# A two-block transformer layer on one core: expert weights in six ring places and six side places, side places used in every pair of experts

## What is computed

```python
def hierarchical_moe(h, w_rg, b_rg, w_re, b_re, w1, w3, w2):
    # per token: the best of 4 groups, in it the best 2 of 8 experts, weights e_w
    ...
    def expert_block(args):
        xb, e = args
        hid = jax.nn.silu(xb @ w1[e]) * (xb @ w3[e])     # 1024 -> 512
        return hid @ w2[e]                               # 512 -> 1024
    ...

def first_block(x, ...):
    ...                                                  # attention and a gated convolution
    h2 = modulate(rms_norm(x, g_norm2[l]), sh2, sc2)
    x = x + ga2[:, None, :] * hierarchical_moe(h2, ...)
    return x

def reference(...):
    x = first_block(...)
    return second_block(x, ...)                          # recurrent mixer, attention, FFN, PLE
```

## Time and profile before

| | before |
|---|---|
| median of 3 runs | 1196.93 us (1193.87 to 1198.81) |
| the profiled execution's span | 1196.8 us, its own time within 0.1 us of the median |
| PE busy | 1148.5 us (96%) |
| DVE, ACT, POOL busy | 481.1, 410.5, 222.0 us |
| moved by DMA | 331.68 MB, mean 277 GB/s |
| chain that ended last | PE 73%, DMA 16%, DVE 6%, issue 2%, ACT 2% |
| largest DMA part of the chain | ring<-in_w (expert weights), 15% |

### The profile page before, as it was taken

The page is one execution under the profiler, slowest core; times in us unless marked ns, Lnnn a source line. Parts: engine busy times, 40 slices in busy tenths (PEclk is TensorE's granted clock), DMA queues, the critical chain, the costliest instruction groups (busy, mean ns, idle before and its releaser), DMA issues.

```text
span 1196.8 us, 15588 instructions
## 1 busy us (share of the span) xinstructions
PE 1148.5 (96%) x5930; PEld 761.6 (64%) x5930; DVE 481.1 (40%) x971; ACT 410.5 (34%) x609; POOL 222.0 (19%) x100
## 2 busy tenths in 40 slices
PE   4999999999999999999989998999999999999998
PEld 2678867774444444444434435978877788888886
DVE  3475552753222222222212215589454653323226
ACT  3533454232111111111111115664245363444334
POOL 0163333300000000000000002200313444443522
PEclk8899999999999999999999998999999999999999
DMA  9897366689899999999999996453223464645541
GB/s 355 322 329 264 128 229 246 269 329 367 339 377 421 423 422 421 422 422 422 422 420 421 422 421 240 160 192 126 86 71 141 150 194 159 210 147 181 201 163 48
DMA packets 92329, 331.68 MB, mean 277 GB/s; under 512 B 3937, under 2 KB 26754, under 8 KB 66674
## 3 DMA queue, kind: packets, MB, share of 16 engines
q1 hardware_dynamic: 91648, 330.36, 71.2%
q0 software_dynamic: 432, 0.48, 0.2%
q10 hardware_dynamic: 194, 0.06, 0.0%
HBM read 329.84 MB, written 1.05 MB: 276 GB/s over the span
## 4 chain that ended last, share of the span: by engine, by line
PE 73%; DMA 16%; DVE 6%; issue 2%; ACT 2%; SPq 0%; DVEq 0%; ACTq 0%
DMA ring<-in_w 15%; PE ps L839 14%; PE ps L840 13%; PE ps L841 13%; PE ps L1196 13%; PE ps L1238 5%; PE ps L1168 1%; PE ps L1169 1%; DVE ring_r L1992 1%; PE ps L912 1%; DMA ring<-in_w_ada 1%; ACT ring_r L1550 1%; PE ps L1349 1%; PE ps L976 1%; PE ps L974 1%
## 5 line engine op out<-in xcount | busy, mean ns | idle before, releaser
L814 POOL TENSOR_TENSOR ring_r<-ring,ring_r 128x1024 fp32r<-128x1024 f32 x76 | 197.8, 2623 | 824.5 <-ACT ring_r L1550 824.4
L1196 PE MATMUL ps<-ring,arena 128*64 128x512 f32 x1008 | 226.0, 596 | 8.8 <-DMA ring<-in_w 7.7
L840 PE MATMUL ps<-ring_r,hl_r 128*128 128x512 f32 x528 | 211.4, 400 | 0.0
L839 PE MATMUL ps<-ring_r,hl_r 128*128 128x512 f32 x480 | 197.5, 411 | 10.7 <-DVE hr_r L2085 6.1
L841 PE MATMUL ps<-ring_r,hr_r 128*128 128x512 f32 x480 | 192.0, 400 | 0.0
L1550 ACT ACTIVATE ring_r<-ring 128x2048 fp32r<-128x2048 f32 x90 | 167.4, 1907 | 62.5 <-PE ps L841 45.0
L1196 PEld LDWEIGHTS ps<-ring,arena 128*64 128x64 f32 x1008 | 69.5, 137 | 149.0 <-issue 127.6
L1992 DVE TENSOR_TENSOR ring_r<-ring,ring_r 128x2048 fp32r<-128x2048 f32 x52 | 121.3, 2339 | 84.5 <-ACT ring_r L1550 84.3
L839 PEld LDWEIGHTS ps<-ring_r,hl_r 128*128 128x128 f32 x480 | 91.8, 191 | 41.2 <-issue 14.7
L840 PEld LDWEIGHTS ps<-ring_r,hl_r 128*128 128x128 f32 x528 | 101.0, 191 | 21.9
L841 PEld LDWEIGHTS ps<-ring_r,hr_r 128*128 128x128 f32 x480 | 91.8, 191 | 22.3
(11 more groups left out here) (370 smaller groups left out, 1650.7 us busy)
## 6 DMA issues: line engine op xcount, KB each, us to landing
ring<-in_w SPq DMA_DIRECT2D x91, 2048.0 KB, 21.5
ring<-in_w_in SPq DMA_DIRECT2D x21, 2048.0 KB, 8.4
ring<-in_w_ada SPq DMA_DIRECT2D x16, 1024.0 KB, 10.2
ring<-in_w_ffn_gate SPq DMA_DIRECT2D x11, 1024.0 KB, 5.2
ring<-in_w_ffn_up SPq DMA_DIRECT2D x11, 1024.0 KB, 7.8
ring<-in_w_ffn_down SPq DMA_DIRECT2D x5, 2048.0 KB, 7.8
ring<-in_w_ada SPq DMA_DIRECT2D x4, 2048.0 KB, 8.7
ring<-in_w_o SPq DMA_DIRECT2D x2, 2048.0 KB, 7.7
```

The costliest lines, as they stand in the source:

```text
L814: nc.gpsimd.tensor_tensor(rest[:, a:b], w[:, a:b], lead[:, a:b].bitcast(F32), ALU.subtract).then_inc(sem("w_rest_b"), 1)
L839: mm(o, lhsT=a_lead, rhs=b_lead, start=start, stop=False, skip_group_check=True)
L840: mm(o, lhsT=a_lead, rhs=b_rest, start=False, stop=False, skip_group_check=True)
L1196: last = mm(H[slots_of(e), :], lhsT=xs[:, k, slots_of(e)], rhs=w, start=k == 0, stop=k == KD - 1)
```

## The change

It touches three engines.

- **Places.** `early_w2` now holds w2 of every even pair, and `early_w1` chunk 0 of every odd pair. In the ring, slots 4, 1 and 2 (chunks 0, 4 and 5) then hold only every other pair's chunk, so there they are free a pair earlier.
- **SP.** The first transfer into `spp` is issued when the router's logits have been read (`small.released["lgt1"]`), ahead of that into `x`, which still waits for the first gather. From pair 3 on, `pair_loads` issues a pair's loads. For pairs 3 to 8 the order is chunks 0, 4, 5, 1, 2, 3, from pair 9 on 0 to 5. Chunks 0, 4 and 5 wait for pair i - 2, chunks 1, 2 and 3 for pair i - 1 as before.
- **PE.** Turns 0 to 11 are one loop of two turns (an even, an odd), run six times; turns 12 to 15 are written out behind the branch.
- **POOL.** The clearing of `scT` waits for `moe_ys1_done` at 15 instead of 3.

```diff
-        BESIDE = {0: (1,), 4: (0, 2), 5: (0, 2)}
+        BESIDE = {0: 1, 4: 0, 5: 0}
...
-            landed[slot] += 16 * (PAIRS - len(BESIDE.get(n, ())))
+            landed[slot] += 16 * (PAIRS // 2 if n in BESIDE else PAIRS)
...
+        def pair_loads(sp_, i, odd, order):
+
+            for n in order:
+                if odd and n == 0:
+                    sp_.wait_ge(*block_used(0, i - 1))
+                    for e in range(2):
+                        early_w1_load(sp_, i, e)
+                elif not odd and n == 4:
+                    sp_.wait_ge(sem("moe_ys1_done"), i - 1)
+                    for e in range(2):
+                        early_w2_load(sp_, i, e)
+                elif odd or n < 4:
+                    sp_.wait_ge(*block_used(n, i - 1 if n in BESIDE else i))
+                    expert_load(sp_, n, i, chunk_in)
...
+            sp_.wait_ge(*small.released["lgt1"])
+            early_w1_load(sp_, 1, 1)
             sp_.wait_ge(sem("moe_gather1_done"), 1)
-            early_w1_load(sp_)
+            early_w1_load(sp_, 1, 0)
...
-            with sp_.Fori(3, PAIRS) as i:
-                for n in range(6):
-                    sp_.wait_ge(*block_used(n, i))
-                    expert_load(sp_, n, i, chunk_in)
+            with sp_.Fori(1, AHEAD_TWOS) as j:
+                for n in (1, 2):
+                    pair_loads(sp_, 2 * j + n, n == 1, (0, 4, 5, 1, 2, 3))
+            with sp_.Fori(AHEAD_TWOS, PAIRS // 2 - 1) as j:
+                for n in (1, 2):
+                    pair_loads(sp_, 2 * j + n, n == 1, range(6))
+            pair_loads(sp_, PAIRS - 1, True, range(6))
...
-            pool.wait_ge(sem("moe_ys1_done"), 3)
+            pool.wait_ge(sem("moe_ys1_done"), PAIRS - 1)
...
                 if early:
-                    pe.wait_ge(sem("early_w2_in"), 64 * early)
+                    pe.wait_ge(sem("early_w2_in"), 64 * half_i + 64)
...
-            turn(0, 0, 0, 1)
-            turn(1, 0, 0)
-            turn(2, 0, 0, 2)
-            with pe.Fori(3, PAIRS - LATE_TURNS) as i:
-                turn(i, 0, 0)
+            with pe.Fori(0, (PAIRS - LATE_TURNS) // 2) as j:
+                turn(2 * j, j, 0, 0, False)
+                turn(2 * j + 1, j, 0, 0, True)
 
             def late_turns():
-                with pe.Fori(PAIRS - LATE_TURNS, PAIRS - 1) as i:
-                    turn(i, 0, 0)
-                last_turn(PAIRS - 1, 0, 0)
+                for i in range(PAIRS - LATE_TURNS, PAIRS - 1):
+                    turn(i, i // 2, 0, 0, i % 2 == 1)
+                last_turn(PAIRS - 1, PAIRS // 2 - 1, 0, 0, True)
```

More of the change, by code:

```diff
@@ L34 @@
 LATE_TURNS = 4
+AHEAD_TWOS = 4
 DFF = 2816
@@ L564, in two_blocks, with in_ring @@
             moe_in_base.append(landed[slot] + 16)
-            landed[slot] += 16 * (PAIRS - len(BESIDE.get(n, ())))
+            landed[slot] += 16 * (PAIRS // 2 if n in BESIDE else PAIRS)
             busy[slot] = sem("moe_" + name), 2 * PAIRS - 1 + n % 2 if n < 4 else PAIRS
-        def in_ring(n, i):
-            beside = BESIDE.get(n, ())
-            return moe_in_base[n] + 16 * (i - (sum(b < i for b in beside) if isinstance(i, int) else len(beside)))
+        def in_ring(n, i, half_i):
+            return moe_in_base[n] + 16 * (half_i if n in BESIDE else i)
         def block_used(n, pairs):
@@ L706, in expert_load, with early_w1_load @@
             sp_.dma_start(view, src).then_inc(signal[MOE_SLOT[n]], 16)
[L708 to L712, removed]
+        def early_w1_load(sp_, pair, e):
+            w = expert_w[0][bass.ds(2 * pair + e, 1)]
+            src = w.rearrange("e (h p j) n -> h p (e j n)", p=P, j=4)
+            sp_.dma_start(early_w1[e], src[0]).then_inc(sem("early_w1_in"), 16)
         def early_w2_load(sp_, pair, e):
-            src = expert_w[4][2 * pair + e].rearrange("(h p j) n -> h p (j n)", p=P, j=2)
+            w = expert_w[4][bass.ds(2 * pair + e, 1)]
+            src = w.rearrange("e (h p j) n -> h p (e j n)", p=P, j=2)
             for h in range(2):
                 sp_.dma_start(early_w2[2 * e + h], src[h]).then_inc(sem("early_w2_in"), 16)
+        def pair_loads(sp_, i, odd, order):
[11 more added lines that the diff above has]
+                    expert_load(sp_, n, i, chunk_in)
         block = ctx.enter_context(nc.Block())
@@ L1173, in slots_of, with chunk_ready @@
                 return slice(e * CAP, (e + 1) * CAP)
-            def chunk_ready(n, i, done):
+            def chunk_ready(n, i, half_i, done):
                 if done:
@@ L1178, in chunk_ready, with up @@
                 else:
-                    pe.wait_ge(chunk_in[MOE_SLOT[n]], in_ring(n, i))
-            def up(n, H, i, done, beside=False):
+                    pe.wait_ge(chunk_in[MOE_SLOT[n]], in_ring(n, i, half_i))
+            def up(n, H, i, half_i, done, odd):
+                beside = odd and n == 0 and not done
                 for h in range(2):
                     if beside and h == 0:
-                        pe.wait_ge(sem("early_w1_in"), 32)
+                        pe.wait_ge(sem("early_w1_in"), 32 * half_i + 32)
                     else:
-                        chunk_ready(2 * n + h, i, done)
+                        chunk_ready(2 * n + h, i, half_i, done)
                     if n == 0:
@@ L1213, in w2_rows, with middle @@
                 return ring[:, MOE_SLOT[4 + f // 2], at:at + COL]
-            def middle(i, done, col0, more_pairs, early=0):
+            def middle(i, half_i, done, col0, more_pairs, odd):
+                early = not odd and not done
                 places(i, done, col0)
-                up(1, HB, i, done)
+                up(1, HB, i, half_i, done, odd)
                 if more_pairs:
@@ L1233, in middle @@
                     if not early:
-                        chunk_ready(4 + h, i, done)
+                        chunk_ready(4 + h, i, half_i, done)
                     for half, Y in enumerate((HA, HB)):
@@ L1260, in first_gather, with turn, last_turn @@
                     gather(n)
-            def turn(i, done, col0, early=0):
-                middle(i, done, col0, True, early)
+            def turn(i, half_i, done, col0, odd):
+                middle(i, half_i, done, col0, True, odd)
                 pe.wait_ge(sem("moe_ys_scaled"), 2 * i + 2 * done + 1)
-                up(0, HA, i + 1, done, early == 1)
+                up(0, HA, i + 1, half_i + odd, done, not odd)
                 combine(i, done)
-            def last_turn(i, done, col0):
-                middle(i, done, col0, False)
+            def last_turn(i, half_i, done, col0, odd):
+                middle(i, half_i, done, col0, False, odd)
                 combine(i, done)
@@ L1274, in _ @@
             more = pe.value_load(flag[0:1, 0:1], min_val=0, max_val=1)
-            up(0, HA, 0, 0)
-            turn(0, 0, 0, 1)
-            turn(1, 0, 0)
-            turn(2, 0, 0, 2)
-            with pe.Fori(3, PAIRS - LATE_TURNS) as i:
-                turn(i, 0, 0)
+            up(0, HA, 0, 0, 0, False)
+            with pe.Fori(0, (PAIRS - LATE_TURNS) // 2) as j:
+                turn(2 * j, j, 0, 0, False)
+                turn(2 * j + 1, j, 0, 0, True)
             def late_turns():
-                with pe.Fori(PAIRS - LATE_TURNS, PAIRS - 1) as i:
-                    turn(i, 0, 0)
-                last_turn(PAIRS - 1, 0, 0)
+                for i in range(PAIRS - LATE_TURNS, PAIRS - 1):
+                    turn(i, i // 2, 0, 0, i % 2 == 1)
+                last_turn(PAIRS - 1, PAIRS // 2 - 1, 0, 0, True)
             with pe.If(more > 0):
@@ L1290, in _ @@
                 first_gather(PAIRS)
-                up(0, HA, 0, PAIRS)
+                up(0, HA, 0, 0, PAIRS, False)
                 with pe.Fori(0, PAIRS * EXTRA_ROUNDS - 1) as i:
-                    turn(i, PAIRS, EXPERTS)
-                last_turn(PAIRS * EXTRA_ROUNDS - 1, PAIRS, EXPERTS)
+                    turn(i, 0, PAIRS, EXPERTS, False)
+                last_turn(PAIRS * EXTRA_ROUNDS - 1, 0, PAIRS, EXPERTS, False)
             with pe.Else():
```

## The result

| | before | after |
|---|---|---|
| median (runs in comparison) | 1195.93 us (4: 1193.87 to 1198.81) | 1187.76 us (4: 1186.25 to 1189.15) |
| ratio, 95% interval | | 0.992, 0.9903 to 0.9937 |
| the profiled run, own time / span | 1198.81 / 1196.8 us | 1187.62 / 1185.7 us |
| expert stage, begin of turn 0 to turn 15 | 430.6 us | 421.3 us |
| last expert chunk lands | 722.3 us | 712.5 us |

The gain is 8.2 us by the medians. The two profiled spans differ by 11.1 us, since the profile of before belongs to the slowest of its runs and that of after to a middling one. The changed kernel, run once more in the experiments on another chip, gave 1188.80 against 1197.93 us: 9.1 us, ratio 0.9925 (0.9911 to 0.9939).

The account below looks back on a forecast made before the run. The prediction took DMA loads of expert weights, 29.8 us a pair against PE's 27.73, to bound the kernel. Standstill falling from 13.5 to 4.7 us wins 8.8: 1196.8 - 8.8 = 1188.0 us, range 1184 to 1195.

Parts of the forecast that it names:

- The bound: Expert stage: DMA sets its end; engines stood still 13.5 us before 360 us, 4.7 after, so loads finish 8.8 us earlier.
- 265 to 275: DMA window in us: loading `spp` earlier cuts a loss of 3.1 us to 1.7.
- 295 to 300: DMA window in us: the queue runs dry earlier, so the loss grows from 1.35 to 2.7 us.
- 322 to 332: DMA window in us where SP waits for slot 4: its loss of 6.6 us vanishes.
- 332 to 360: DMA window in us: of a loss of 2.45 us, 0.3 is left for seams.
- The order of the loads: SP's loads from pair 3: chunk 0, then two w2 chunks, find free places early and keep DMA busy to about 359 us.
- The rival of gaps that move and are not filled: SP's fixed order lets one late place hold all behind it: gain 0 to 5 us, about 1193.5 us; chance 0.10.
- Where the stall goes: PE's wait for weights moves from L1196 in turns 8 to 14 to w2 in turn 14, from 12.9 to about 4 us.
- Turn 15 and the tail: End of the stage: turn 15 begins at 699.7 us, and the stage ends 8.5 us behind the last chunk, at 722.0.
- Span and own time: Whole program: profiled span 1196.8 less 8.8 gives 1188.0 us, the median taken as 0.1 above that span.
- Rival 1: PE's back branch over two turns misses its code, five times 1.72 us: gain 4.4, time 1192.5 us; chance 0.12.
- Rivals 2 and 3: 2: three code packets late each round, 1209.8 us, chance 0.08 with all else slower; 3: gaps move unfilled, about 1193.5, chance 0.10.

Follow-up runs that it names:

- e8: The change with turns and loads written out, chunk 1 of pair 5 loaded only in part (output not the reference's): 1183.53 against 1197.93 us, ratio 0.9878.
- e2: The change with `spp` loaded late again, behind the first gather and `x`: 1189.10 against 1197.33 us, ratio 0.992.
- e1: The change with its side places, but pairs 3 to 8 also load chunks in the order 0 to 5: 1194.91 against 1197.33 us, ratio 0.9977.
- e5: The change written out without loops, natural order, w2 side places only in pairs 0 and 2: 1195.87 against 1197.36 us, ratio 0.9982.
- e6: The change written out without loops, natural order, chunk 0 side place only in pair 1: 1197.50 us, ratio 1.0003 to before.
- e10: The change with w2's side places given back by halves through a new semaphore: 1185.73 against 1197.36 us, ratio 0.990.
- e12: The changed kernel itself, run again as control on another chip: 1188.80 against 1197.93 us, ratio 0.9925.
- e3: The change with PE's turns and SP's loads written out in place of loops: 1190.66 against 1197.33 us, ratio 0.9935.
- e9: The change with PE's loop holding six turns, run twice, in place of two turns run six times: 1190.81 against 1197.93 us, ratio 0.9939.
- e7: The change with the order 0, 4, 5, 1, 2, 3 kept for all pairs from 3 to 15: 1196.95 against 1197.36 us, ratio 1.0000.
- e4: The change written out without loops, side places and changed order only up to pair 6: 1190.15 against 1197.33 us, ratio 0.9931.
- e11: The kernel with w2's places given back by halves, PE also waiting for each half of w2 separately: 1187.04 against 1197.93 us, ratio 0.9903.

## Why the prediction was right, and where its steps were off

It said 1188.0 us, faster; the median is 1187.76. Step by step:

- **The bound.** Right. DMA time lost before 360 us was the price of the stage: 13.5 us before, 4.7 foreseen, 4.3 measured. The last chunk landed 9.8 us earlier, 8.8 foreseen; 0.4 of the difference is the gaps, and the rest the rate behind 360 us, which was 422 against 421. e8 confirms it from the other side. The forecast was right here by its mechanism and not by luck: the gap that it said would go went, and nothing stood still behind it.
- **The gaps one by one.** 265 to 275: 1.3 left (1.7 foreseen). 295 to 300: 2.5 (2.7). 322 to 332: none, and 332 to 360: none (0.3 left for seams). A loss of 0.5 at 275 to 295 was not foreseen. `spp` early wins nothing: right, e2.
- **The order of the loads.** The forecast worked out which chunk finds a free place when, but took side places and order as one step and priced neither alone. In the natural order both kinds of place are worth 2.4 us (e1), chunk 0's alone 1.5 (e5) and w2's alone nothing (e6); with the order both win 8 to 9. The rival of gaps that move and are not filled came true in e1 and e5 (in e6 the gap stays where it was), not in the change.
- **Where the stall goes.** Right in place, off in size: w2 of turn 14 waited 1.96 us, not the "about 4" (4.7 by the prediction's own 699.7 - 695.0). Its last transfer came at 682.70 and not at 683.7, and PE was later there, since the waits on w1 and w3 did not vanish but became small: 4.8 us in six (PEld), with one of 0.83 on PE in turn 13. The whole loss of PE was 3.6 us.
- **Turn 15 and the tail.** Turn 15 at 698.54 (699.7 foreseen, so "699 to 701" was missed by 0.5). Block 2 came 7.4 us behind the last chunk and not 8.5. This is the mis-sized term: the 8.5 of before held a stretch of low clock in its last pair, 0.89 and 0.77 in two windows, in which w2 took 8.78 us. After, the same work took 3.65 + 0.23 + 3.65 at full clock. That is an accident of the one profile of each, not a gain of the change: e10, which holds the whole change, has the stretch in turn 15 again (8.5 us from landing to block 2), e12 has not (7.3). I should have read the clock beside the tail:

```profile
715.00:720.00 5.00, 3.36 (x16) 0.89 1.00 417
720.00:725.00 5.00, 5.00 (x20) 0.77 1.04 386
```

(windows of the kernel before), and after, for the like stretch:

```profile
710.00:714.00 4.00, 3.77 (x20) 1.00 1.03 389
```

- **Span and own time.** The one plain slip. The prediction took the profiled execution's time as within 0.1 us of the median, since its span reads 1196.8. But a run's own time stands about 1.9 us above its span (1187.62 and 1185.7 after), and the profiled run of before was the one of 1198.81. The sum should have read 1198.8 - 8.8 = 1190.0 for a run like that one. The slip did no harm by luck: the span of that slow run happens to read as the median of the three runs, 1196.93, and for a median the sum is 1196.93 - 8.8 = 1188.1. That the forecast met 1187.76 within 0.3 us is luck too: the median of before then came out 1.0 lower (1195.93), and the gain 0.6 smaller. The gain itself, 8.8 against 8.2 and 9.1, was sized well; the 11.1 between the two profiles is the 9.8 of the landing and the 1.1 of the tail, with 0.2 behind it.
- **Rival 1.** Refuted at two turns, by the change itself and by e3. Between those at 308.3 and 609.3 us no instruction packet of 16 KB came. Of the two statements in the Trainium skill ("Runtime: NRT & Kernel Launch", section Instruction fetch mechanics) the one of 128 KiB for PE agrees with 41 KB staying; a body of some 124 KB by our estimate, just under that figure, did not stay, so it seems that not the whole 128 KiB served it (e9). Where the limit lies was not tried. By the two-page window the loop of two turns would have fetched.
- **Rivals 2 and 3.** Neither appeared.

What lies behind the stage took 465.8 us (466.0 before), so it moved up whole.

## What to carry to other kernels

Where one queue issues the loads in a fixed order, look at the order in which places come free before adding buffers; here the new places alone, in the old order, won 2.4 of some 9 us. Such an order is good only while there is a lead, and must end before the lead does, or the consumer waits for what it needs first although the transfers are done as early (e7). Give a place back by the pieces in which it is used: that cost one semaphore (e10) and was worth 2 to 3 us by the ratios to before, at the edge of what the intervals tell apart, where using the side places behind pair 6 was worth nothing (e4).

## What was unexpected of the hardware

- **The clock behind short waits of PE.** After a wait of 1.0 to 2.1 us in turn 14, the granted clock fell to its lower level (1.2 GHz, 0.5) for 3.4 us in e1, e2, e3, e6, e8 and e9, and did not in the change or e12, where the wait was just as long:

```profile
682.00:686.00 4.00, 3.30 (x16) 1.00 1.01 426
```

It costs about 1.7 us a time. e11 met it behind the branch's gap of 1.56 us, e4 in turn 13 behind 2.30, e6 also in turn 10 behind 1.96. In turn 15 before, e1, e2, e5, e7 and e10 had such a stretch and the other eight profiles none. At the begin of block 2 all had one but e6 and e8, whose rest of the program took 463.9 and 464.1 us against 465.5 to 466.0 in all others. Runs of one kernel spread by up to 9.5 us (e1), and this is a part of it: the six runs of e12 go from 1186.46 us at a mean clock of 0.993 to 1191.42 at 0.987. What decides was not found. A difference of 1.7 us between two single profiles should be looked for here first.
- **Code fetched on the way and the DMA rate.** Between 400 and 680 us the six kernels that fetch PE code all along (e3, e4, e5, e6, e8, e9) moved 420.4 to 421.4 GB/s beside their instruction packets, and the seven with the loop of two turns 422.3 to 422.5. But the kernel before loops too and moved 421.5. It uses side places in no pair from 3 on, and like is better compared with like: e4, with few side places too, moved 420.4 (1.1 less than before), and e3, e8 and e9, with all of them, 420.9 to 421.4 (1.0 to 1.5 less than after). Some 0.5 of it is the room that the packets take themselves. This is a correlation, no cause is shown; it is worth about 1 us over the stage.
- **A far branch when the DMA engines are full.** The one ahead of turn 12 left PE idle for 1.56 us after, 1.72 before and 1.17 to 1.76 over all fourteen profiles, the back branch of e9 1.64, all at some 422 GB/s of other traffic. No run has such a branch with the DMA engines idle.
